# First mixer of a two-block transformer: level products in four bursts with bank regions of their own, chunk states in the other bank, two weight remainders on GpSimd

## The reference, cut to what matters

```
q, f, i, g = split(h @ w_in, 4)
fg = lb + (1 - lb) * sigmoid(f)
S_t = diag(fg_t) S_(t-1) + (1 - fg_t) i_t^T          # per head
o_t = S_t^T silu(q_t)
o = o * rsqrt(mean(o^2) + eps) * g_norm * silu(g)
mix = o @ w_out
```

## Time and profile before

| | us |
|---|---|
| runs, median (lowest to highest) | 1484.4 (1484.1 to 1485.28) |
| profiled execution, its own span from first to last instruction | 1483.1 |
| around the span (median minus span) | 1.3 |
| busy PE / PEld | 1452.5 (98%) / 1207.6 (81%) |
| busy DVE / ACT / POOL | 859.6 (58%) / 615.7 (42%) / 482.5 (33%) |
| mixer, four head pairs | about 44 to 262 of the span |

### The profile page before, as it was taken

How to read it: one execution, slowest core, us unless ns; L and a number is a source line. 1 busy time by engine, 2 the same in 40 slices (tenths; PEclk the granted TensorE clock), 3 DMA queues, 4 the chain that set the end, 5 groups by cost and what they waited for, 6 DMA issues and landing times.

```text
span 1483.1 us, 23698 instructions
## 1 busy us (share of the span) xinstructions
PE 1452.5 (98%) x9390; PEld 1207.6 (81%) x9390; DVE 859.6 (58%) x1261; ACT 615.7 (42%) x780; POOL 482.5 (33%) x360
## 2 busy tenths in 40 slices
PE   8999999999999999999999999999999999999999
PEld 6787887898888888899777988888888897777677
DVE  7787686576665660165686666656630374565741
ACT  5565554353223221245574442232221355655541
POOL 0000000225544545432221145445454524422222
PEclk9999999999999999999999999999999999999999
DMA  7422122403222233323102122222323312322211
GB/s 222 136 74 87 58 86 102 156 29 114 85 92 106 87 112 113 112 87 106 66 30 86 57 86 85 95 103 88 110 85 112 129 58 86 130 74 71 72 56 59
DMA packets 23601, 137.25 MB, mean 93 GB/s; under 512 B 2600, under 2 KB 5208, under 8 KB 8672
## 3 DMA queue, kind: packets, MB, share of 16 engines
q1 hardware_dynamic: 18288, 124.79, 23.9%
q10 hardware_dynamic: 5232, 11.32, 2.8%
HBM read 131.89 MB, written 4.21 MB: 92 GB/s over the span
## 4 chain that ended last, share of the span: by engine, by line
issue 41%; PE 27%; POOL 24%; DVE 3%; DMA 2%; ACT 1%; DVEq 1%; POOLq 0%; ACTq 0%; SPq 0%
POOL WL L468 15%; POOL WL L477 9%; PE pair L503 7%; PE pair L505 6%; PE pair L504 6%; DMA RAW<-stream 1%; PE pair L1096 1%; PE pair L1083 1%; DVE WL L1672 1%; PE pair L688 1%; PE pair L1015 1%; PE pair L1073 1%; PE pair L717 1%; ACT WH L1202 1%; DMA PAR<-params 0%
## 5 line engine op out<-in xcount | busy, mean ns | idle before, releaser
L503 PE MATMUL pair<-AH,WH 128*128 128x512 f32 (+1 forms) x1240 | 473.4, 382 | 9.4 <-DVE AL L1661 6.6
L468 POOL TENSOR_TENSOR WL<-RAW,WH 128x512 fp32r<-128x512 f32 x228 | 310.5, 1394 | 475.6 <-ACT WH L1202 475.6
L505 PE MATMUL pair<-AH,WL 128*128 128x512 f32 (+1 forms) x1240 | 462.6, 373 | 0.0
L504 PE MATMUL pair<-AL,WH 128*128 128x512 f32 (+1 forms) x1240 | 462.4, 373 | 0.0
L1202 ACT ACTIVATE WH<-RAW 128x2048 fp32r<-128x2048 f32 x106 | 202.8, 1913 | 455.5 <-PE pair L505 446.4
L477 POOL TENSOR_TENSOR WL<-RAW,WH 128x512 fp32r<-128x512 f32 x128 | 171.8, 1374 | 506.8 <-ACT WH L1202 506.8
L503 PEld LDWEIGHTS pair<-AH,WH 128*128 128x128 f32 x1240 | 233.5, 188 | 58.5 <-issue 15.9
L505 PEld LDWEIGHTS pair<-AH,WL 128*128 128x128 f32 x1240 | 233.0, 188 | 41.8
L504 PEld LDWEIGHTS pair<-AL,WH 128*128 128x128 f32 x1240 | 233.5, 188 | 41.1 <-issue 1.9
L2042 DVE TENSOR_SCALAR CA<-pair,PAR 128x512 f32<-128x512 f32 x88 | 67.3, 806 | 147.4 <-PE pair L505 144.4
L503 PE MATMUL pair<-GH,WH 128*128 (+2 forms) x416 | 148.7, 357 | 0.1
(11 more groups left out here) (249 smaller groups left out, 1890.4 us busy)
## 6 DMA issues: line engine op xcount, KB each, us to landing
RAW<-stream SPq DMA_DIRECT2D x114, 1024.0 KB, 4.9
H<-x_t SPq DMA_DIRECT2D x5, 512.0 KB, 6.6
bias_rows<-ROWS ACTq DMA_DIRECT2D x1, 2048.0 KB, 24.5
BIAS<-bias_rows ACTq DMA_DIRECT2D x1, 2048.0 KB, 7.8
FBC<-forget_rows ACTq DMA_DIRECT2D x4, 512.0 KB, 4.0
out<-H ACTq DMA_DIRECT2D x8, 256.0 KB, 2.0
H<-x_t SPq DMA_DIRECT2D x1, 1024.0 KB, 10.4
RAW<-stream SPq DMA_DIRECT2D x3, 256.0 KB, 6.7
```

Of the source, the lines that this page charges most:

```text
L468: pool.tensor_tensor(WL[w][:, part], RAW[raw][:, part], WH[w][:, part].bitcast(F32), ALU.subtract).then_inc(w_lo, 1)
L503: pe.matmul(out_, wh, xh, start=start, stop=False, skip_group_check=shared)
L504: pe.matmul(out_, wh, xl, start=False, stop=False, skip_group_check=shared)
L505: return pe.matmul(out_, wl, xh, start=False, stop=stop, skip_group_check=shared)
```

## The change

PE's order: gate pieces 0 and 1 come first, then levels 0 and 1 together; gate 2, the turn of KD, gate 3; then levels 2, 3 and 7 and the chunk states together; two forget pieces; levels 4 and 5 together; two forget pieces; level 6; four query pieces; outputs. Levels 2, 3 and 7 write columns 0, 128 and 256 of pair_a, levels 4 and 5 columns 0 and 128 of it, level 6 pair_b; the chunk states go from pair_a to pair_b. DVE picks 2, 3 and 7 in a row, and 4 and 5 in a row, and waits for the end of a burst (`LV_DONE`); level 6 is the last level, so the four copies to SS follow its pick. DVE makes the remainder of the next f chunk (and, in the first pair, KD) ahead of pick 0, and the next v chunk's ahead of pick 6; pick 6 stands ahead of the scan. ACT takes exponent 5 ahead of `gate`. The remainders of chunks 16 and 17 are POOL's.

```diff
--- before.py
+++ after.py
@@ -344,7 +344,18 @@
         HG_G = [N_HG + 3 + 4 * it for it in range(4)]
-        BY_DVE = range(1, N_HO + 2)
+        BY_DVE = range(1, N_HO)
+        LV_ORDER = (0, 1, 2, 3, LEVELS, 4, 5, 6)
+        LV_PAIR = {0: 3, 1: 2, 2: 2, 3: 2, LEVELS: 2, 4: 2, 5: 2, 6: 3}
+        LV_COL = {2: 0, 3: P, LEVELS: 2 * P, 4: 0, 5: P, 6: 0}
+        LV_DONE = {0: 1, 1: 2, 2: 5, 3: 5, LEVELS: 5, 4: 7, 5: 7, 6: 8}
+        def nth(lv):
+            return LV_ORDER.index(lv) + 1
@@ -353,7 +364,7 @@
-            return 4 * (n + (-1 - N_HO - (extras_before(n) if skip is None else skip)))
+            return 4 * (n + (1 - N_HO - (extras_before(n) if skip is None else skip)))
@@ -485,7 +496,7 @@
-            span(split_rows, N_HO + 2, 2)
+            span(split_rows, N_HO, 4)
             span(split_cols, N_F0 + 2, FB - 2)
@@ -509,7 +520,7 @@
                 elif isinstance(n, int) and n in BY_DVE:
-                    if part % 2 == 0 or n >= N_HO:
+                    if part % 2 == 0:
                         pe.wait_ge(hg_lo, 2 * (n - 1) + part // 2 + 1)
@@ -670,7 +681,7 @@
                 def level(lv):
-                    out_ = pair_b if lv in (0, 3, 4, 6) else pair_a
+                    out_ = bank[LV_PAIR[lv]]
                     if lv < LEVELS:
@@ -685,7 +696,7 @@
                                 for b in range(0, P, BLK):
-                                    mm = pe.matmul(out_[b:b + BLK, h, c * BLK:c * BLK + BLK], k_[:, b:b + BLK], q_[:, b:b + BLK], start=True, stop=True)
+                                    mm = pe.matmul(out_[b:b + BLK, h, LV_COL[lv] + c * BLK:LV_COL[lv] + c * BLK + BLK], k_[:, b:b + BLK], q_[:, b:b + BLK], start=True, stop=True)
                     mm.then_inc(level_mm, 1)
@@ -699,10 +710,9 @@
                     pe.wait_ge(v_copied, it + 1)
-                    pe.wait_ge(level_picked, 8 * it + 3)
                     for h in range(2):
                         for c in range(TT - 1):
-                            mm = pe.matmul(pair_a[:, h, c * P:c * P + P], KD[:, h, c * P:c * P + P],
+                            mm = pe.matmul(pair_b[:, h, c * P:c * P + P], KD[:, h, c * P:c * P + P],
                                            vv[:, c, h * P:h * P + P], start=True, stop=True)
@@ -756,49 +766,38 @@
                 gate(0)
+                gate(1)
                 if it:
                     pe.wait_ge(o_rstd, it)
+                    pe.wait_ge(o_free, it)
                 else:
...
                 level(0)
-                gate(1)
-                if it:
-                    pe.wait_ge(o_free, it)
                 level(1)
...
                 gate(3)
-                pe.wait_ge(level_picked, 8 * it + 2)
+                pe.wait_ge(level_picked, 8 * it + nth(1))
                 level(2)
-                if not last:
-                    forget(0)
-                pe.wait_ge(kd_copied, it + 1)
                 level(3)
+                level(LEVELS)
+                chunk_states()
                 if last:
                     mixed(0, 2)
-                else:
-                    forget(1)
-                chunk_states()
-                if last:
                     mixed(0, 3)
                 else:
-                    forget(2)
-                pe.wait_ge(level_picked, 8 * it + 4)
+                    forget(0)
+                    forget(1)
+                pe.wait_ge(level_picked, 8 * it + nth(LEVELS))
                 level(4)
-                if not last:
-                    forget(3)
-                pe.wait_ge(state_made, it + 1)
                 level(5)
...
                 else:
-                    query(0)
-                pe.wait_ge(level_picked, 8 * it + 5)
+                    forget(2)
+                    forget(3)
+                pe.wait_ge(state_made, it + 1)
                 level(6)
-                if not last:
-                    query(1)
-                pe.wait_ge(level_picked, 8 * it + 6)
-                level(7)
                 if last:
@@ -808,6 +807,8 @@
                 else:
+                    query(0)
+                    query(1)
                     query(2)
@@ -1302,8 +1303,8 @@
                 expo(it, 4)
+                expo(it, 5)
                 gate(it)
-                expo(it, 5)
                 split_hg(HG_G[it])
@@ -1662,14 +1663,10 @@
-                if n in BY_DVE:
-                    dve.wait_ge(w_hi, hi_done(n))
-                    raw, wh, wl = RAW[n % 2][:, :], WH[n % 2][:, :], WL[n % 2][:, :]
-                    if n >= N_HO:
-                        raw, wh, wl = (a.rearrange("p (k c) -> p k c", k=2) for a in (raw, wh, wl))
-                    for half in range(2):
-                        part = (slice(None), slice(None), slice(512 * half, 512 * half + 512)) if n >= N_HO else (slice(None), slice(1024 * half, 1024 * half + 1024))
-                        dve.tensor_tensor(wl[part], raw[part], wh[part].bitcast(F32), ALU.subtract).then_inc(hg_lo, 1)
+                dve.wait_ge(w_hi, hi_done(n))
+                for half in range(2):
+                    part = slice(1024 * half, 1024 * half + 1024)
+                    dve.tensor_tensor(WL[n % 2][:, part], RAW[n % 2][:, part], WH[n % 2][:, part].bitcast(F32), ALU.subtract).then_inc(hg_lo, 1)
@@ -1735,9 +1732,9 @@
             def pick(it, lv):
-                b = 3 if lv in (0, 3, 4, 6) else 2
+                b = LV_PAIR[lv]
                 dve.drain()
-                dve.wait_ge(level_mm, 8 * it + lv + 1)
+                dve.wait_ge(level_mm, 8 * it + LV_DONE[lv])
                 dve.memset(PAD[:, :], 0.0)
@@ -1749,11 +1746,11 @@
                     mask = MASK[:, lv - 2].bitcast(U32).unsqueeze(1).broadcast_to([P, 2, P])
-                    sums, kept = bank[b][:, :, 0:P], SB[:, :, :]
+                    sums, kept = bank[b][:, :, LV_COL[lv]:LV_COL[lv] + P], SB[:, :, :]
                     if lv < LEVELS:
...
                     ins = dve.copy_predicated(kept, mask, sums)
-                if lv == LEVELS:
+                if lv == LV_ORDER[-1]:
                     dve.drain()
@@ -1766,12 +1763,12 @@
                 dve.wait_ge(kv_mm, it + 1)
-                dve.tensor_copy(ST[:, :, 0:P], bank[2][:, :, 0:P])
+                dve.tensor_copy(ST[:, :, 0:P], bank[3][:, :, 0:P])
                 for c in range(1, TT - 1):
...
                         ins = dve.scalar_tensor_tensor(ST[:, h, c * P:c * P + P], ST[:, h, (c - 1) * P:c * P],
-                                                       EB[:, h, c * P + P - 1:c * P + P], bank[2][:, h, c * P:c * P + P],
+                                                       EB[:, h, c * P + P - 1:c * P + P], bank[3][:, h, c * P:c * P + P],
                                                        ALU.mult, ALU.add)
@@ -1800,39 +1797,38 @@
             def hgrn(it, last):
-                pick(it, 0)
                 if it == 0:
                     query_decay(0)
-                split_lo(HG_F[it + 1] if not last else N_HO)
+                if not last:
+                    split_lo(HG_F[it + 1])
                 if it == 0:
                     key_decay(0)
+                pick(it, 0)
                 shift(it, 3)
...
                 scale_qk(it, 3)
+                shift(it, 5)
                 pick(it, 2)
-                shift(it, 5)
+                pick(it, 3)
+                pick(it, LEVELS)
                 scale_qk(it, 4)
-                pick(it, 3)
+                shift(it, 6)
+                scale_qk(it, 5)
                 states(it)
...
                     split_lo(HG_Q[it + 1])
-                shift(it, 6)
-                scale_qk(it, 5)
                 pick(it, 4)
+                pick(it, 5)
                 scale_qk(it, 6)
...
                     forget(it + 1)
-                pick(it, 5)
-                split_lo(HG_V[it + 1] if not last else N_HO + 1)
+                    split_lo(HG_V[it + 1])
+                pick(it, 6)
                 if not last:
                     scan(it + 1)
-                pick(it, 6)
-                if not last:
                     shift(it + 1, 0)
-                pick(it, 7)
-                if not last:
                     shift(it + 1, 1)
...
                     scale_qk(it + 1, 0)
```

## The result

The changed kernel takes 1495.3 us (median of four runs, 1493.1 to 1495.7) against 1484.3 for the kernel before (four runs, 1483.8 to 1485.3) on the same chip: a ratio of 1.0064, with a 95% interval from 1.0052 to 1.0077. The medians are 11.0 us apart, where 4.5 was forecast (by the ratio it is 9.5 us, with 7.7 as the lower end), and the time lies above the range. The profiled execution is the fastest of the four (1493.13 us, its span 1491.3).

A forecast was written before the change was run, and what follows sets the result against it. TensorE (PE) was taken to bound the kernel. First pair 3.2, pairs 2 and 3 0.9, last pair 0 and clock 0.4 sum to +4.5 us on 1484.4: forecast 1488.9 us, range 1482.5 to 1493.5.

The forecast's parts named there:

- the middle pairs: Pairs 2 and 3: PE waits 1.9 us for ACT's square before the head sums, each pair 0.45 us longer.
- The rival that ACT's row is not late: Square before the head sums: it starts 1.9 us earlier than worked out, total 1480.8 us; chance 0.12.
- +3.2: First pair: later turn of KD and a wait before level 3 put the head sums 3.2 us later.
- Net 0: Last pair: a gain of 1.7 us at the outputs, cancelled by a charge of 1.7 us for GpSimd's interference.
- I charge these 1.7: Last pair: VectorE loses 1.7 us beside GpSimd's subtraction for chunk 17; bounds 0 and 3.8.
- outputs at 27.75: Last pair: outputs 27.75 us after its start, before the charge for GpSimd; a gain of 1.7 us.
- The rival with a chance of 0.08: Last pair: three VectorE instructions each wait for a whole GpSimd one, 1.3 us each, 3.8 us, total 1491.0; chance 0.08.
- I add 0.4 us: Clock: 0.4 us added for falls behind the new waits, those in first and last pairs mostly hidden behind DVE.
- falls at each wait for the square: Rival, head sums of the first three pairs: the clock falls each time, 3 x 1.5 us more, 1493.4; chance 0.12.

The follow-up runs named there:

- the run with another phase: The changed kernel with 32 more calls of a tiny matmul, whose result nobody reads, ahead of the mixer: 1497.6 us (one run).
- pick 0 first: The changed kernel, but in the first pair the pick of level 0 stands ahead of the two remainders and KD: 1494.5 us, ratio 1.0074.

## Why the prediction was wrong, and where it was right

The direction was right and so were the middle pairs; the sum was too small. At the last outputs the profiled execution is 9.6 us late where the terms give 4.5. The difference of 5.1 is 1.0 in the first pair, 1.6 in the third (the clock) and 2.9 in the last, less the 0.4 that the sum had for the clock.

**Right: the middle pair.** The place of pick 6 ahead of the scan makes ACT's row 0.84 us later (forecast 0.8), PE waits 2.0 to 2.1 for the square (forecast 1.9), and a pair is 0.47 longer (forecast 0.45). The experiment with the scan first takes that one cause away, and the wait and the loss go with it. The rival that ACT's row is not late is out. PE's own row became 1.7 us shorter up to the sums (1.5 forecast).

**Right in its parts: the first pair.** The turn starts at 56.04 (55.8 forecast), the wait before level 3 is 1.55 (1.8), and the sums are 4.0 later where +3.2 was forecast. Of that difference 0.52 is the first stop at issue, for which the sum had no term.

**Wrong: "Net 0" in the last pair.** It costs 2.9 us (29.44 to 32.34, start to outputs). The main failed step is a term that the sum does not have, the stop at issue inside the burst: 2.46 us. VectorE's picks wait for the end of that burst (3.45 us idle at 247.47), so the stop is passed on whole. The other is the size of "I charge these 1.7": with the remainders back on VectorE the stretch from the stop to level 5 is 2.15 us shorter, so the charge was 0.45 too small. The two make up the whole 2.9. The rest of the step came out as forecast. Without the stop (1.83 there) and without GpSimd the outputs would come 29.51 - 1.83 = 27.7 after the start of the pair, and the prediction's "outputs at 27.75", the gain of 1.7, is the same. The wait stood before level 5 (2.45) and not before level 6 (0.57), because the stop made VectorE late and the group met an earlier scaling. In the run with another phase, where the last pair has no stop, the group begins just as late in the pair (21.5 us after its start in both), VectorE's scaling of level 5 is done by then, and the wait is before level 6, as forecast.

The charge took a loss of 1.74 per group from the earlier trace rows. What the traces show goes by instructions. In the rows before, two of VectorE's met the group. In GpSimd's second group of the changed kernel two met it again, the two of level 5's scaling, and lost 1.1 us each. In the kernel before with the remainders alone four met it, which lost 4.0, and the step costs +4.3 us there. The rival with a chance of 0.08, that each instruction met waits for a whole one of GpSimd's, has the right form, but not its sum of 3.8: two met the group and not three, at 1.1 and not at 1.3. The Trainium skill (page "SBUF — State Buffer", section "Who interferes with whom") says that two such instructions exclude each other for a whole length. The 1.1 us per instruction agree in kind, while the copy from PSUM beside the same group kept its 0.42, as the page has it too. So does the first group, where VectorE's instructions lost nothing and one of GpSimd's took 4.09 us.

**Wrong: "I add 0.4 us" for the clock.** In the profiled execution the clock fell behind the third sums (1.5 us) and in the last pair, where it cost nothing, since VectorE set the pace. By their lower mean clocks it was low for longer in the other three. The experiments with an unchanged middle pair show how uncertain this is: the same wait of 2.0 to 2.1 us left the clock at 1 at 160.36, and in the executions with the remainders on VectorE and with pick 0 first it was followed by a fall at both the second and the third sums. Five traces have this wait three times each. In 6 of the 15 cases the clock fell behind it, and never behind the first sums. The rival "falls at each wait for the square" was thus partly right. The median is 2.1 us above the profiled execution, at lower mean clocks, about what one or two more falls cost; where they lay in the runs without a trace isn't known.

**Not foreseen: the stop in a long burst.** Levels 2, 3 and 7 in a row are 192 matmuls and 192 weight loads within 1.8 us (3 x 0.59). In the last pair PE stops at 244.55 and goes on at 247.00. In the window from 244.4 to 246 of the changed kernel's transfers stands one packet of instructions, which begins at 244.6:

```profile
q8 instruction: 1, 0.02, 3.4%
```

At every stop at issue in these traces PE went on 2.3 to 2.7 us after such a packet of 16 KB began (60.9 and 63.60 here; 242.1 and 244.40 with the scan first). The Trainium skill (page "Runtime: NRT & Kernel Launch", section "Instruction fetch mechanics") says that an engine is refilled in blocks of 16 KiB, 256 instructions, and that this is mostly hidden. The packets agree in size (58 in all, 0.95 MB). Hidden they are in the kernel before, which has as many of them and no stop at issue in its mixer. In the joined burst 384 instructions go by in 1.8 us, less than the 2.3 to 2.7 us from the start of a packet to PE going on, and then it shows. The run with another phase moved the stops from the first and last pairs into the middle ones, which shows that the place in the stream decides. That the packet itself is what PE waits for is not shown; it rests on the times beside each other.

Left open: why the same wait of 2.1 us is followed by a fall of the clock in one execution and not in the next, how much of the first pair with the scan first is due to it, and why the totals with pick 0 first and with the remainders on VectorE do not show the gains that their traces have.

## What to carry to other kernels

When bursts are joined, look at what the engines behind them were given to do in exchange: here one pick and four small copies ahead of a scan cost all that the bursts saved. Before work is moved to GpSimd, look for what VectorE does with two SBUF inputs meanwhile. Count the instructions that the group meets, at up to 1.1 us each at this size, rather than a share of the group; where GpSimd is the one held up, the loss is its own. And where PE is the bound at 98%, a wait of 2 us costs more than 2 us in some executions, since the clock may fall behind it.

## What was unexpected of the hardware

A burst of 192 matmuls of 128x32 with their weight loads can stop in its middle for a reason that lies in the instruction stream: 0.5 to 2.5 us of stop, depending on where it falls in the stream, in or right behind four of the eight such bursts of two kernels (the changed one, and it with another phase). Adding 128 instructions far in front of the bursts changed which ones stopped. That PE outruns its own instruction supply there fits the times of the packets and is argued, not shown.

VectorE and GpSimd can hold each other up in either direction. Beside VectorE GpSimd's remainders took up to 1.78 us each in the second group, and one took 4.09 in the first, against 1.31 alone. In the kernel before with the remainders alone the first group shows both: one of GpSimd's took 3.86, and later two of VectorE's took 1.57 and 1.76, which made PE wait for nothing. What decides which of the two loses is not shown by these runs.
